# Second MLP of a two-stack block on one Trainium2 core: one 512-column matmul in place of two of 256 for the high weights

## Chip, core and metric

One core of a Trainium2 chip. The time is the device time of one execution in microseconds (us). The kernel before has three timed runs with a median of 1813.36 us.

## What is computed

The reference runs 272 tokens (16 meta tokens and 256 of input) of width 1024 through a stack of layers: a state-space mixer and an MLP, latent attention and a second MLP, then on the last 256 tokens an mLSTM mixer, cross attention, a gated MLP, a second kind of self-attention, cross attention and a gated MLP. All inputs are float32. The part that matters here is the second MLP:

```python
def sqrelu_mlp(h, w_up, w_down):
    return jnp.square(jax.nn.relu(h @ w_up)) @ w_down
h = h + sqrelu_mlp(rms_norm(h, ln_mlp[i]), mlp_w_up[i], mlp_w_down[i])
```

with `w_up` of 1024 x 4096 and `w_down` of 4096 x 1024. For i = 1 it is computed for 256 tokens only.

## The kernel before

**Layout.** Features lie on the 128 partitions and tokens in the free dimension, so the residual `X` is 8 chunks of 128 x 272. All weights come from HBM once, in blocks of up to 128 x 1024 (512 KB): 8 chunks of a 128 x 128 stationary operand that together give one output chunk of 128 features.

**Float32 out of reduced matmuls.** TensorE multiplies in a reduced float format (`F32R`). Each operand is split into a high part, which is the value rounded to that format, and a low part, the rest. A product is then high x high + high weight x low operand + low weight x high operand. For the weights ScalarE copies `RAW` to `WH` (a copy that rounds) and VectorE subtracts, `WL = RAW - WH`. For the operand, ScalarE writes `HNH` or `ASH` and VectorE `HNL` or `ASL`. `HNH/HNL` hold the normed input of the up projection (8 chunks), `ASH/ASL` the squared relu (16 chunks, two quarters of the hidden layer).

**One list of blocks.** `PLAN` is a list of all 514 weight blocks in the order of their use, and every engine's program walks it. SyncE loads block j into `RAW[j % 4]` as soon as `WL` of j-4 is written. ScalarE's `act_split` keeps three blocks ahead (`LEAD`), VectorE's `dve_split` two (`LEAD_LO`), into `WH` and `WL` with four buffers each. `pe_block` waits for the bank (one of three, i % 3, free once the eviction of block i-3 is done), for `WL` of its block and for each operand chunk, and then issues 24 matmuls with 256 (or 272) columns, three for each of 8 chunks:

```python
                q.matmul(o, wh, xh, k == 0, False)
                q.matmul(o, wh, xl, False, False)
                t = q.matmul(o, wl, xh, False, k == kc - 1)
```

The operand's part is the moving one, and the weights are the stationary one, loaded ahead of each matmul.

**The MLP.** The hidden layer is done in four quarters of 8 blocks. `mlp_order` gives the order: up 0, up 1, down 0, up 2, down 1, up 3, down 2, down 3, in all 64 blocks. In this text block n is the n-th of them, so up 0 is blocks 0 to 7 and down 0 is blocks 16 to 23. The order of each engine's instructions is that of its function's loop (`pe_mlp`, `act_mlp`, `dve_mlp`, `pool_mlp`), and each engine takes them strictly in order:

- Up block: ScalarE first splits a later block (`WH`), then waits for the matmuls and writes relu of the bank into `TMP[n % 4]`, which frees the bank. GpSimd squares `TMP` in place. ScalarE rounds it to `ASH` (`act_part`), VectorE writes `ASL` (`dve_part`). VectorE's order in a block: `WL` of a later block, then `ASL` of this one.
- Down block: VectorE writes `WL` of a later block, waits for the matmuls and multiplies the bank by the row `RR2` (the square of 1/rms, since the norm's scale is applied only here) into `TMP[6 + n % 2]`, which frees the bank. GpSimd adds that to `X`. VectorE waits for the add of two down blocks earlier before it writes into the same `TMP`.
- Up 0 also ends the norm: the sum of squares comes from TensorE behind block 0, ScalarE makes a rough 1/rms with Ln and Exp, and VectorE refines it (`dve_newton`, L171) and squares it into `RR2`.
- Down 3 also begins the next norm: `act_norm`, `dve_norm` and GpSimd's sums of pairs of squares.

The profile names the helper's line for every instruction: L140 is a matmul, L149 an activation, L159 `tensor_tensor`, L171 `scalar_tensor_tensor`, L180 `tensor_reduce`, L189 a DMA. So instructions are told apart by their tiles.

Of the kernel before, what the change touches and what calls it, by code (L numbers as in the profile page):

```python
# [5 lines left out]
ALU = mybir.AluOpType  # L6
# [5 lines left out]
T1 = 272  # L12
T2 = 256
# [186 lines left out]
def build_program(nc, cpack, xin, memin, W, out):  # L200
    with ExitStack() as ctx:

        def sb(name, shape, dt=F32):
            return ctx.enter_context(nc.sbuf_tensor(name, shape, dt))
# [6 lines left out]
        def sig(name):  # L211
            sigs.append(Sig(sem(name)))
            return sigs[-1]
# [26 lines left out]
        def row(n, T):  # L240
            return Rbuf[:, n, 0:T]
# [78 lines left out]
        def pe_block(q, name, r, m, T, xs):  # L320
            i = q.block(name, r, m)
            pe_bank_free(q, i)
            q.wait_ge(*lo[i])
            o = bank_of(i)[:, 0:T]
            kc = KC[name]
            for k in range(kc):
                xh, xl, ready = xs[k]
                wh = WH[:, i % NWS, k * 128:(k + 1) * 128]
                wl = WL[:, i % NWS, k * 128:(k + 1) * 128]
                q.wait_ge(*ready)  # L330
# [3 lines that stand above are left out]
                if k == kc - 1:  # L334
                    t.then_inc(*use(i))

        def act_block(q, name, r, m, T):
            i = q.block(name, r, m)
            act_split(q, i)
            return i, bank_of(i)[:, 0:T]  # L340
# [6 lines left out]
        def hn_chunks(key):  # L347
            T = NORMS[key][3]
            return [(HNH[:, c, 0:T], HNL[:, c, 0:T], hn[key, c]) for c in range(8)]

        def as_chunks(tag, c0, n, T, by=1):
            return [(ASH[:, c0 + c, 0:T], ASL[:, c0 + c, 0:T], al[tag, c // by]) for c in range(n)]
# [583 lines left out]
        r2 = sig("r_squared")  # L936
        sqr = sig("relu_squared")
        xadd = sig("x_added")

        MT = (T1, T2)  # L940

# [6 lines left out]
        def mlp_order():  # L948
            return [("up", 0), ("up", 1), ("down", 0), ("up", 2), ("down", 1), ("up", 3), ("down", 2), ("down", 3)]

        def pe_mlp(q, l, nxt):
            key = f"mlp{l}"
            xs = hn_chunks(key)
            for kind, q4 in mlp_order():
                for m in range(8):
                    if kind == "up":
                        pe_block(q, f"up{l}", 0, 8 * q4 + m, MT[l], xs)
                        if q4 == 0 and m == 0:
                            pe_rest(q, key, MT[l])
                    else:  # L960
                        pe_block(q, f"down{l}", q4, m, MT[l], as_chunks(("up", l, q4), q4 % 2 * 8, 8, MT[l]))
                        if q4 == 3:
                            pe_feed(q, nxt, m, NORMS[nxt][3], rms[key])

        def act_mlp(q, l, nxt):
            key, T = f"mlp{l}", MT[l]
            for kind, q4 in mlp_order():
                if kind == "down" and q4 == 3:
                    q.table(LOGS)
                for m in range(8):  # L970
                    if kind == "up":
                        n, c = 8 * q4 + m, q4 % 2 * 8 + m
                        i, b = act_block(q, f"up{l}", 0, n, T)
                        if n == 0:
                            act_table(q, key, row(RST, T), T, 1024,
                                      evd[AT["ssd", 0, 47]] if l == 0 else evd[AT["mlain", 0, 2]])
                        v = TMP[:, n % 4, 0:T]
                        q.wait_ge(*use[i])
                        if n >= 4:
                            q.wait_ge(*al[("up", l, (n - 4) // 8), (n - 4) % 8])  # L980
                        q.activation(v, b, ACT.Relu).then_inc(*eva(i))
                        act_part(q, ("up", l, q4), m, ASH[:, c, 0:T], v, up_free(l, q4), sqr[l, n])
                    else:
                        i, b = act_block(q, f"down{l}", q4, m, T)
                        if q4 == 3:
                            act_norm(q, nxt, m, xadd[l, 3, m], use[AT[f"up{l}", 0, 31]])

        def dve_mlp(q, l, nxt):
            key, T = f"mlp{l}", MT[l]
            for kind, q4 in mlp_order():  # L990
                for m in range(8):
                    if kind == "up":
                        n, c = 8 * q4 + m, q4 % 2 * 8 + m
                        if n == 0:
                            dve_norm(q, key, 7)
                        i, b = dve_block(q, f"up{l}", 0, n, T)
                        if n == 0:
                            r = row(RST, T)
                            dve_newton(q, key, r, SUMS[:, 0:T], 1024, rough[key])
                            q.wait_ge(*rms[key])  # L1000
                            if l:
                                q.wait_ge(*evd[AT["down0", 3, 7]])
                            q.tt(row(RR2, T), r, r, ALU.mult).then_inc(*r2(l))
                        dve_part(q, ("up", l, q4), m, ASL[:, c, 0:T], TMP[:, n % 4, 0:T], ASH[:, c, 0:T])
                    else:
# [3 lines left out]
                        q.wait_ge(*r2[l])  # L1009
                        if n >= 2:  # L1010
                            q.wait_ge(*xadd[l, (n - 2) // 8, (n - 2) % 8])
                        q.tt(TMP[:, 6 + n % 2, 0:T], b, row(RR2, T), ALU.mult).then_inc(*evd(i))
                        if q4 == 3 and m:
                            dve_norm(q, nxt, m - 1)

        def pool_mlp(q, l, nxt):
            T, t0 = MT[l], T1 - MT[l]
            for kind, q4 in mlp_order():
                for m in range(8):
                    if kind == "up":  # L1020
                        n = 8 * q4 + m
                        v = TMP[:, n % 4, 0:T]
                        q.wait_ge(*eva[AT[f"up{l}", 0, n]])
                        q.tt(v, v, v, ALU.mult).then_inc(*sqr(l, n))
                    else:
                        n = 8 * q4 + m
                        q.wait_ge(*evd[AT[f"down{l}", q4, m]])
# [4 lines left out]
                        q.tt(X[:, m, t0:T1], X[:, m, t0:T1], TMP[:, 6 + n % 2, 0:T], ALU.add).then_inc(*xadd(l, q4, m))  # L1032
                        if q4 == 3:
                            pool_pair(q, nxt, m, NORMS[nxt][3])

# [1693 lines left out]
```

## Time and profile before

| | |
|---|---|
| timed runs | 1811.76, 1813.36, 1814.75 us; median 1813.36 |
| the profiled execution | 1816.08 us, of which the span of the instructions is 1814.3 |
| TensorE | 1728.0 us busy (95%), 13396 matmuls; granted clock 0.965 in the mean |
| VectorE | 1193.6 us (66%), 2054 instructions |
| ScalarE | 934.8 us (52%), 1640 |
| GpSimd | 316.0 us (17%), 281 |
| HBM read | 254.29 MB, 141 GB/s over the span |
| second MLP | from about 700 us (first matmuls) to 884 us (last add to X) of the span |

Times of rows are in microseconds from the start of the span, PE is TensorE, DVE VectorE, ACT ScalarE, POOL GpSimd. A row of the timeline has the start, the duration, the engine, the line, the operation, what is written and what is read, and in brackets how long the engine had been idle before it and whom it waited for. A duration runs to the end of an instruction's last write, and the next instruction can start before that.

### The profile page before, as it was taken

How to read it: one execution, taken by the hardware profiler on the slowest of the kernel's cores; microseconds unless marked ns; L12 is line 12 of the kernel's file. 1: busy time of each engine (PE TensorE's matmuls, PEld its weight loads, DVE VectorE, ACT ScalarE, POOL GpSimd, SP SyncE). 2: the span in 40 equal slices, each digit the busy share in tenths (PEclk: the TensorE clock that was granted, in tenths of full speed). 3: DMA queues.
4: the chain of work that ended last, by engine and by line, in shares of the span. 5: the costliest groups of instructions: out<-in, count | busy, mean ns of one | idle time of the engine just before them, and what ended most of it. 6: DMA issues, size and time to landing. Idle time of an engine off the chain costs nothing.

```text
span 1814.3 us, 33107 instructions
## 1 busy us (share of the span) xinstructions
PE 1728.0 (95%) x13396; PEld 1659.1 (91%) x13396; DVE 1193.6 (66%) x2054; ACT 934.8 (52%) x1640; POOL 316.0 (17%) x281
## 2 busy tenths in 40 slices
PE   6999999999988999999999999999989999989997
PEld 6999889999986989999988999999989998889997
DVE  5899987555576446555766675776666766466665
ACT  5677765544443445544655444544445654354443
POOL 0000001233420002333211100000241211010025
PEclk8999999999998779999999999999999999999998
DMA  5333334555522116555533544455553343335553
GB/s 186 120 114 105 117 103 140 163 176 173 179 79 79 44 57 189 194 187 186 164 116 117 180 146 129 140 183 187 183 169 116 113 156 117 99 123 175 188 179 109
DMA packets 76328, 257.49 MB, mean 142 GB/s; under 512 B 8464, under 2 KB 12560, under 8 KB 75920
## 3 DMA queue, kind: packets, MB, share of 16 engines
q1 hardware_dynamic: 76176, 255.37, 43.9%
q8 instruction: 107, 1.75, 0.4%
q14 instruction: 45, 0.37, 0.1%
HBM read 254.29 MB, written 1.05 MB: 141 GB/s over the span
## 4 chain that ended last, share of the span: by engine, by line
PE 78%; DVE 11%; ACT 5%; issue 4%; POOL 1%; DMA 0%; POOLq 0%; DVEq 0%; ACTq 0%; SPq 0%
PE pb L140 77%; DVE WL L159 2%; DVE TMP L171 2%; DVE SCR L171 2%; DVE SCR L159 2%; PE pb L143 1%; ACT SCR L149 1%; ACT L156 1%; POOL SCR L159 1%; ACT WH L149 1%; DVE HNL L171 1%; ACT TMP L149 1%; ACT Rbuf L149 0%; ACT SCR L150 0%; DVE MX L180 0%
## 5 line engine op out<-in xcount | busy, mean ns | idle before, releaser
L140 PE MATMUL pb<-HNH,WH 128*128 128x256 f32 (+1 forms) x2176 | 632.8, 291 | 3.6 <-DVE WL L159 3.5
L140 PE MATMUL pb<-HNH,WL 128*128 128x256 f32 (+1 forms) x2176 | 621.7, 286 | 0.0
L140 PE MATMUL pb<-HNL,WH 128*128 128x256 f32 (+1 forms) x2176 | 621.2, 285 | 0.0
L159 DVE TENSOR_TENSOR WL<-RAW,WH 128x1024 fp32r<-128x1024 f32 (+4 forms) x514 | 602.5, 1174 | 6.8 <-ACT WH L149 6.1
L149 ACT ACTIVATE WH<-RAW 128x1024 fp32r<-128x1024 f32 (+4 forms) x514 | 507.4, 989 | 170.5 <-PE pb L140 169.0
L140 PE MATMUL pb<-ASH,WH 128*128 128x256 f32 (+1 forms) x1632 | 479.0, 294 | 3.2 <-DVE ASL L171 1.8
L140 PE MATMUL pb<-ASH,WL 128*128 128x256 f32 (+1 forms) x1632 | 469.3, 288 | 0.0
L140 PE MATMUL pb<-ASL,WH 128*128 128x256 f32 (+1 forms) x1632 | 468.8, 287 | 0.0
L140 PEld LDWEIGHTS pb<-HNH,WH 128*128 128x128 f32 x2176 | 415.6, 191 | 10.4 <-issue 4.7
L140 PEld LDWEIGHTS pb<-HNH,WL 128*128 128x128 f32 x2176 | 415.6, 191 | 0.0
L140 PEld LDWEIGHTS pb<-HNL,WH 128*128 128x128 f32 x2176 | 414.2, 190 | 1.1
L140 PEld LDWEIGHTS pb<-ASH,WH 128*128 128x128 f32 x1632 | 315.7, 193 | 10.6 <-issue 5.3
L140 PEld LDWEIGHTS pb<-ASL,WH 128*128 128x128 f32 x1632 | 315.0, 193 | 1.0
L140 PEld LDWEIGHTS pb<-ASH,WL 128*128 128x128 f32 x1632 | 315.7, 193 | 0.0
L140 PE MATMUL pb<-SCR 128*64 128x128 f32 (+11 forms) x928 | 136.2, 319 | 15.5 <-DVE SCR L171 9.5
L140 PEld LDWEIGHTS pb<-SCR 128*128 128x128 f32 (+5 forms) x928 | 105.7, 173 | 36.1 <-DVE SCR L171 11.2
L159 DVE TENSOR_TENSOR ASL<-TMP,ASH 128x256 fp32r<-128x256 f32 (+1 forms) x108 | 46.4, 430 | 109.2 <-ACT ASH L149 109.2
L140 PE MATMUL pb<-SQ,cp 128*128 128x256 f32 (+2 forms) x274 | 85.6, 428 | 33.5 <-ACT SQ L149 24.0
L159 POOL TENSOR_TENSOR SCR<-SCR,TMP 128x256 f32<-128x256 f32 x48 | 59.9, 1248 | 311.7 <-DVE TMP L159 311.7
L159 POOL TENSOR_TENSOR X<-X,TMP 128x272 f32<-128x272 f32 (+1 forms) x64 | 96.4, 1507 | 87.9 <-DVE TMP L159 87.9
L159 DVE TENSOR_TENSOR TMP<-pb,Rbuf 128x256 f32<-128x256 f32 (+1 forms) x112 | 47.9, 428 | 94.8 <-PE pb L140 94.8
L149 ACT ACTIVATE ASH<-TMP 128x256 fp32r<-128x256 f32 (+1 forms) x108 | 45.5, 422 | 117.2 <-DVE TMP L159 67.6
(136 smaller groups left out, 1484.8 us busy)
## 6 DMA issues: line engine op xcount, KB each, us to landing
RAW<-in_w_gu SPq DMA_DIRECT2D x88, 512.0 KB, 4.1
RAW<-in_w_up SPq DMA_DIRECT2D x64, 512.0 KB, 3.5
RAW<-in_w_down SPq DMA_DIRECT2D x64, 512.0 KB, 3.6
RAW<-in_w_ssd SPq DMA_DIRECT2D x48, 512.0 KB, 3.5
RAW<-in_w_xkv SPq DMA_DIRECT2D x32, 512.0 KB, 3.5
RAW<-in_w_mlin SPq DMA_DIRECT2D x24, 512.0 KB, 3.5
RAW<-in_w_fd SPq DMA_DIRECT2D x32, 384.0 KB, 3.0
RAW<-in_w_sbqkv SPq DMA_DIRECT2D x24, 512.0 KB, 3.9
```

The source lines that it names most:

```text
L140: return self.eng.matmul(o, l, r, start=start, stop=stop, skip_group_check=skip) if self.eng else Nothing()
L143: return self.eng.transpose(o, i, ident) if self.eng else Nothing()
L149: return self.eng.activation(o, i, f, bias=bias, scale=scale)
L156: self.eng.preload_act_table_set(name)
L159: return self.eng.tensor_tensor(o, a, b, op) if self.eng else Nothing()
L171: return self.eng.scalar_tensor_tensor(out=o, in0=a, scalar=s, in1=b, op0=op0, op1=op1)
```

## The change

In the second MLP (l = 1) the up blocks and the down blocks of quarters 0 to 2 take another form; the first MLP and down 3 stay.

- `HNH/HNL` become the two halves of one tile `HN[:, chunk, 0 or 1, token]`, and `ASH/ASL` those of `AS`, so that the high and the low part of a chunk lie 272 columns apart.
- `pe_wide_block`: for each chunk one matmul of 512 columns with the stationary `WH`, whose moving operand is the high part and then the low part, 256 columns each, into both halves of the bank; then one of 256 columns with `WL` and the high part, into the first half. So 16 matmuls a block instead of 24, and the block's result is the sum of the bank's halves.
- Whoever reads the bank adds the halves. That is VectorE with a `tensor_reduce` over a view of the bank whose last dimension has two elements, 256 apart.
- Up block: VectorE does that reduction into `TMP`, which now frees the bank; ScalarE then does relu in place in `TMP`, GpSimd's square follows. `ASH` and `ASL` of block n are written one block later (`act_square_part`, `dve_square_part` of n-1, after the relu and the reduction of n), except at a quarter's last block, which ScalarE writes in the same block and VectorE at the start of the next group.
- Down block (quarters 0 to 2): the reduction takes the place of VectorE's product with `RR2`; GpSimd multiplies by `RR2` in place, waits for its own product, and then adds to `X`.

The core of the diff:

```diff
-        HNH = sb("HNH", [128, 8, T1], F32R)
-        HNL = sb("HNL", [128, 8, T1], F32R)
-        ASH = sb("ASH", [128, 16, T1], F32R)
-        ASL = sb("ASL", [128, 16, T1], F32R)
+        HN = sb("HN", [128, 8, 2, T1], F32R)
+        AS = sb("AS", [128, 16, 2, T1], F32R)
+        HNH, HNL = HN[:, :, 0, :], HN[:, :, 1, :]
+        ASH, ASL = AS[:, :, 0, :], AS[:, :, 1, :]
...
-                q.wait_ge(*(eva if PLAN[i - 3][0] in ("up0", "up1", "wk") else evd)[i - 3])
+                q.wait_ge(*(eva if PLAN[i - 3][0] in ("up0", "wk") else evd)[i - 3])
...
+        def pe_wide_block(q, name, r, m, xs):
...
+            for k in range(kc):
+                x, ready = xs[k]
+                q.wait_ge(*ready)
+                q.matmul(o[:, :].rearrange("p (a t) -> p a t", a=2), WH[:, i % NWS, k * 128:(k + 1) * 128], x[:, :, 0:T2],
+                         k == 0, False, True)
+                t = q.matmul(o[:, 0:T2], WL[:, i % NWS, k * 128:(k + 1) * 128], x[:, 0, 0:T2], False, k == kc - 1, True)
+            t.then_inc(*use(i))
+
+        def halves(b):
+            return b[:, :].rearrange("p (a t) -> p t a", a=2)
...
                         v = TMP[:, n % 4, 0:T]
-                        q.wait_ge(*use[i])
-                        if n >= 4:
-                            q.wait_ge(*al[("up", l, (n - 4) // 8), (n - 4) % 8])
-                        q.activation(v, b, ACT.Relu).then_inc(*eva(i))
-                        act_part(q, ("up", l, q4), m, ASH[:, c, 0:T], v, up_free(l, q4), sqr[l, n])
+                        if l:
+                            q.wait_ge(*evd[i])
+                            q.activation(v, v, ACT.Relu).then_inc(*relu(n))
...
+                            if m:
+                                act_square_part(q, l, n - 1)
+                            if m == 7:
+                                act_square_part(q, l, n)
...
-                        dve_part(q, ("up", l, q4), m, ASL[:, c, 0:T], TMP[:, n % 4, 0:T], ASH[:, c, 0:T])
+                        v = TMP[:, n % 4, 0:T]
+                        if l:
+                            q.wait_ge(*use[i])
+                            if n >= 4:
+                                q.wait_ge(*al[("up", l, (n - 4) // 8), (n - 4) % 8])
+                            q.red(v, halves(bank_of(i)), ALU.add, False).then_inc(*evd(i))
+                        if l == 0:
+                            dve_square_part(q, l, n)
+                        elif m or q4 == 1:
+                            dve_square_part(q, l, n - 1)
                     else:
                         i, b = dve_block(q, f"down{l}", q4, m, T)
+                        if l and m == 0 and q4 < 3:
+                            dve_square_part(q, l, 15 if q4 == 0 else 8 * q4 + 15)
...
+                        if down_wide(l, q4):
+                            q.red(v, halves(bank_of(i)), ALU.add, False).then_inc(*evd(i))
+                        else:
+                            q.wait_ge(*r2[l])
+                            q.tt(v, b, row(RR2, T), ALU.mult).then_inc(*evd(i))
...
+                        if down_wide(l, q4):
+                            q.wait_ge(*r2[l])
+                            q.tt(v, v, row(RR2, T), ALU.mult).then_inc(*scaled(q4, m))
+                            q.wait_ge(*scaled[q4, m])
```

## Rows read from the trace of the kernel before

**Rows 1.** The chain that ended last, in order of time, 700 to 890 us: start, us, what.

```profile
by line: PE pb L140 100.1%
...
699.95 190.11 PE pb L140 x1595
```

**Rows 2.** Two stretches: us, then PE, PEld, DVE, ACT, POOL busy, PEclk, DMA share, GB/s.

```profile
716.00:860.00 144.00, 144.00 (x1219) 144.00 (x1218) 79.46 (x103) 73.22 (x107) 54.71 (x51) 1.00 0.58 188
900.00:960.00 60.00, 55.57 (x426) 52.90 (x427) 38.94 (x68) 32.78 (x51) 6.80 (x5) 1.00 0.39 124
```

**Rows 3.** Timeline of PE: first matmul of blocks 3 and 17 (start us, us).

```profile
709.05 0.28 PE L140 MATMUL pb<-HNH,WH 128*128 128x256 f32 x1
...
748.81 0.28 PE L140 MATMUL pb<-ASH,WH 128*128 128x256 f32 x1
```

**Rows 4.** Timeline of DVE, up blocks: start us, us, what [idle before].

```profile
781.81 0.43 DVE L159 TENSOR_TENSOR ASL<-TMP,ASH 128x256 fp32r<-128x256 f32 x1 [1.28 <-ACT ASH L149]
782.15 1.22 DVE L159 TENSOR_TENSOR WL<-RAW,WH 128x1024 fp32r<-128x1024 f32 x1
```

**Rows 5.** Timeline of DVE, the turn from up to down blocks.

```profile
748.07 1.22 DVE L159 TENSOR_TENSOR WL<-RAW,WH 128x1024 fp32r<-128x1024 f32 x1
749.21 0.42 DVE L159 TENSOR_TENSOR TMP<-pb,Rbuf 128x256 f32<-128x256 f32 x1
```

**Rows 6.** Timeline of PE: V projection, first and last of 24 matmuls of 512 columns.

```profile
563.70 0.39 PE L140 MATMUL pb<-WH,ASH 128*128 128x512 f32 x1
...
569.03 0.40 PE L140 MATMUL pb<-WL,ASH 128*128 128x512 f32 x1
```

**Rows 7.** Timeline of ACT: the norm before block 1, and one up block.

```profile
704.08 0.42 ACT L149 ACTIVATE Rbuf<-Rbuf 128x256 f32<-128x256 f32 x1
...
780.25 0.38 ACT L149 ACTIVATE TMP<-pb 128x256 f32<-128x256 f32 x1 [0.36 <-PE pb L140]
781.36 0.42 ACT L149 ACTIVATE ASH<-TMP 128x256 fp32r<-128x256 f32 x1 [0.72 <-POOL TMP L159]
781.68 1.04 ACT L149 ACTIVATE WH<-RAW 128x1024 fp32r<-128x1024 f32 x1
```

**Rows 8.** Groups of DVE over the whole run: xcount | busy us, mean ns.

```profile
L180 DVE TENSOR_REDUCE SCR<-pb 128x1 f32<-128x272 f32 x16 | 6.9, 430 | 0.0
L180 DVE TENSOR_REDUCE MX<-pb 128x2 f32<-128x512 f32 x8 | 5.5, 691 | 5.0 <-PE pb L140 5.0
L171 DVE SCALAR_TENSOR_TENSOR SCR<-pb,cp 128x512 f32<-128x512 f32 x8 | 6.0, 750 | 10.2 <-PE pb L140 10.2
```

**Rows 9.** Timeline of POOL: the square of block 0, and one in up 2.

```profile
704.85 0.61 POOL L159 TENSOR_TENSOR TMP<-TMP 128x256 f32<-128x256 f32 x1 [8.97 <-ACT TMP L149]
...
780.71 0.61 POOL L159 TENSOR_TENSOR TMP<-TMP 128x256 f32<-128x256 f32 x1 [2.23 <-ACT TMP L149]
```

**Rows 10.** Timeline of DVE: the Newton step before the first eviction.

```profile
704.99 0.75 DVE L171 SCALAR_TENSOR_TENSOR TMP<-TMP,Rbuf 128x256 f32<-128x256 f32 x1
705.78 0.43 DVE L171 SCALAR_TENSOR_TENSOR Rbuf<-TMP,Rbuf 128x256 f32<-128x256 f32 x1
...
706.58 0.42 DVE L159 TENSOR_TENSOR ASL<-TMP,ASH 128x256 fp32r<-128x256 f32 x1
```

**Rows 11.** Timeline of DVE in down 3.

```profile
869.03 1.76 DVE L159 TENSOR_TENSOR WL<-RAW,WH 128x1024 fp32r<-128x1024 f32 x1
```

**Rows 12.** Timeline of POOL: adds to X in down 0 and down 3.

```profile
749.71 1.65 POOL L159 TENSOR_TENSOR X<-X,TMP 128x256 f32<-128x256 f32 x1 [2.46 <-DVE TMP L159]
...
868.79 0.91 POOL L159 TENSOR_TENSOR X<-X,TMP 128x256 f32<-128x256 f32 x1 [0.24 <-DVE TMP L159]
```

**Rows 13.** DMA issues: xcount, KB each, median us from issue to landing.

```profile
RAW<-in_w_up SPq DMA_DIRECT2D x64, 512.0 KB, 3.5
```

More of the change, by code:

```diff
@@ L335, in pe_block @@
                     t.then_inc(*use(i))
+        def pe_wide_block(q, name, r, m, xs):
+            i = q.block(name, r, m)
+            pe_bank_free(q, i)
+            q.wait_ge(*lo[i])
+            o = bank_of(i)
+            kc = KC[name]
+            for k in range(kc):
[7 more added lines that the diff above has]
+            return b[:, :].rearrange("p (a t) -> p t a", a=2)
         def act_block(q, name, r, m, T):
@@ L349, in hn_chunks, with hn_wide, as_wide @@
             return [(HNH[:, c, 0:T], HNL[:, c, 0:T], hn[key, c]) for c in range(8)]
+        def hn_wide(key):
+            return [(HN[:, c], hn[key, c]) for c in range(8)]
+        def as_wide(tag, c0, n, by=1):
+            return [(AS[:, c0 + c], al[tag, c // by]) for c in range(n)]
         def as_chunks(tag, c0, n, T, by=1):
@@ L938, in build_program @@
         xadd = sig("x_added")
+        relu, scaled = sig("relu"), sig("down_scaled")
         MT = (T1, T2)
@@ L949, in mlp_order, with down_wide @@
             return [("up", 0), ("up", 1), ("down", 0), ("up", 2), ("down", 1), ("up", 3), ("down", 2), ("down", 3)]
+        def down_wide(l, q4):
+            return l == 1 and q4 < 3
         def pe_mlp(q, l, nxt):
             key = f"mlp{l}"
-            xs = hn_chunks(key)
+            xs = hn_wide(key) if l else hn_chunks(key)
             for kind, q4 in mlp_order():
@@ L956, in pe_mlp @@
                     if kind == "up":
-                        pe_block(q, f"up{l}", 0, 8 * q4 + m, MT[l], xs)
+                        if l:
+                            pe_wide_block(q, "up1", 0, 8 * q4 + m, xs)
+                        else:
+                            pe_block(q, "up0", 0, 8 * q4 + m, T1, xs)
                         if q4 == 0 and m == 0:
                             pe_rest(q, key, MT[l])
+                    elif down_wide(l, q4):
+                        pe_wide_block(q, "down1", q4, m, as_wide(("up", l, q4), q4 % 2 * 8, 8))
                     else:
@@ L963, in pe_mlp, with act_square_part, dve_square_part @@
                             pe_feed(q, nxt, m, NORMS[nxt][3], rms[key])
+        def act_square_part(q, l, n):
+            q4, m = divmod(n, 8)
+            act_part(q, ("up", l, q4), m, ASH[:, q4 % 2 * 8 + m, 0:MT[l]], TMP[:, n % 4, 0:MT[l]], up_free(l, q4), sqr[l, n])
+        def dve_square_part(q, l, n):
+            q4, m = divmod(n, 8)
+            c = q4 % 2 * 8 + m
+            dve_part(q, ("up", l, q4), m, ASL[:, c, 0:MT[l]], TMP[:, n % 4, 0:MT[l]], ASH[:, c, 0:MT[l]])
         def act_mlp(q, l, nxt):
@@ L971, in act_mlp @@
                     if kind == "up":
[L972 removed]
+                        n = 8 * q4 + m
                         i, b = act_block(q, f"up{l}", 0, n, T)
@@ L992, in dve_mlp @@
                     if kind == "up":
-                        n, c = 8 * q4 + m, q4 % 2 * 8 + m
+                        n = 8 * q4 + m
                         if n == 0:
@@ L1003, in dve_mlp @@
                             q.tt(row(RR2, T), r, r, ALU.mult).then_inc(*r2(l))
-                        dve_part(q, ("up", l, q4), m, ASL[:, c, 0:T], TMP[:, n % 4, 0:T], ASH[:, c, 0:T])
+                        v = TMP[:, n % 4, 0:T]
+                        if l:
+                            q.wait_ge(*use[i])
+                            if n >= 4:
+                                q.wait_ge(*al[("up", l, (n - 4) // 8), (n - 4) % 8])
+                            q.red(v, halves(bank_of(i)), ALU.add, False).then_inc(*evd(i))
+                        if l == 0:
+                            dve_square_part(q, l, n)
+                        elif m or q4 == 1:
+                            dve_square_part(q, l, n - 1)
                     else:
                         i, b = dve_block(q, f"down{l}", q4, m, T)
+                        if l and m == 0 and q4 < 3:
+                            dve_square_part(q, l, 15 if q4 == 0 else 8 * q4 + 15)
                         n = 8 * q4 + m
                         q.wait_ge(*use[i])
-                        q.wait_ge(*r2[l])
                         if n >= 2:
                             q.wait_ge(*xadd[l, (n - 2) // 8, (n - 2) % 8])
-                        q.tt(TMP[:, 6 + n % 2, 0:T], b, row(RR2, T), ALU.mult).then_inc(*evd(i))
+                        v = TMP[:, 6 + n % 2, 0:T]
+                        if down_wide(l, q4):
+                            q.red(v, halves(bank_of(i)), ALU.add, False).then_inc(*evd(i))
+                        else:
+                            q.wait_ge(*r2[l])
+                            q.tt(v, b, row(RR2, T), ALU.mult).then_inc(*evd(i))
                         if q4 == 3 and m:
@@ L1022, in pool_mlp @@
                         v = TMP[:, n % 4, 0:T]
-                        q.wait_ge(*eva[AT[f"up{l}", 0, n]])
+                        q.wait_ge(*(relu[n] if l else eva[AT["up0", 0, n]]))
                         q.tt(v, v, v, ALU.mult).then_inc(*sqr(l, n))
@@ L1026, in pool_mlp @@
                         n = 8 * q4 + m
+                        v = TMP[:, 6 + n % 2, 0:T]
                         q.wait_ge(*evd[AT[f"down{l}", q4, m]])
+                        if down_wide(l, q4):
+                            q.wait_ge(*r2[l])
+                            q.tt(v, v, row(RR2, T), ALU.mult).then_inc(*scaled(q4, m))
+                            q.wait_ge(*scaled[q4, m])
                         if q4:
@@ L1031, in pool_mlp @@
                             q.wait_ge(*evd[AT["ssdo", 1, m] if l == 0 else AT["mlao", 0, m]])
-                        q.tt(X[:, m, t0:T1], X[:, m, t0:T1], TMP[:, 6 + n % 2, 0:T], ALU.add).then_inc(*xadd(l, q4, m))
+                        q.tt(X[:, m, t0:T1], X[:, m, t0:T1], v, ALU.add).then_inc(*xadd(l, q4, m))
                         if q4 == 3:
```

4 lines of the change are left out of this document (added).

## The prediction

> **What bounds the kernel now.** I read the page first, then the chain of waits over the second MLP, then that stage's timeline engine by engine. The chain runs on TensorE alone for 190 us [rows 1], and TensorE is busy in all of 716 to 860 us at a granted clock of 1.00, that is at 2.4 GHz, while VectorE works 55% of it and ScalarE 51% [rows 2]. So only TensorE's own time, or something that newly holds it up, can move the result. The stage has 64 blocks: 32 up, 32 down. One block is 24 matmuls of 256 columns. From the first matmul of block 3 (709.05) to the first of block 17 (748.81) there are 14 blocks [rows 3], so a block takes 39.76 / 14 = 2.84 us and a matmul 118.3 ns. The 0.28 in these rows is how long one takes from end to end; successive matmuls overlap.
>
> VectorE's rows show how much room it has: in an up block it subtracts WL (1.22 us), then sits idle for 1.28 us until ScalarE's ASH, then writes ASL (0.42) [rows 4]. The eviction is ScalarE's, and VectorE is not in it. In a row of VectorE the next instruction starts before the last ends: ASL at 781.81 and WL at 782.15 are 0.34 apart, and WL 748.07 to TMP 749.21 is 1.14 [rows 4, 5]. I use 0.34, 1.14 and a lead of 0.08 us.
>
> **The change on TensorE.** 56 blocks (32 up, 24 down) turn two 256-column matmuls per chunk into one of 512: eight pairs a block. The 512-column matmuls of this trace are those of the V projection: from 563.70 to 569.03 there are 23 steps [rows 6], 231.7 ns each. The pair costs 236.6 ns now. Eight times 4.9 ns is 0.04 us a block, so a block takes 2.80 us, and 56 blocks save 2.2 us. That is all that TensorE gives: the columns stay the same, and the only thing saved is a fixed share per matmul. The bounds are 0 (the same rate per column) and, since 512 columns at 2.4 GHz need 213 ns, 8 x (236.6 - 213.3) = 0.19 us a block or 10.4 us; I take the row, because it is the same width with its weights loaded each time. The Trainium skill (TensorE: Matmul & The Clock Gate, Back-to-back issue gap) puts the gap at N/2.4 + 2.5 ns: by it a pair would save 2.5 ns and the stage 1.1 us. The rows don't follow it, neither at 256 columns (118.3) nor at 512 (231.7).
>
> **The change off TensorE.** In an up block ScalarE's relu out of the bank (0.38) becomes VectorE's reduction of 512 elements into TMP, then a relu from TMP to TMP, which I price at 0.42 as ScalarE's other SBUF copies of 256 [rows 7]. No row has a reduction of pairs; the reduction of 512 bank elements into two takes 691 ns, of 272 into one 430 [rows 8]. So it goes by elements read, and I take 0.69, occupying VectorE for 0.61. Bounds: 0.60, and 1.22, the price of 1,024 elements, should each of the 256 outputs cost something. In a down block the reduction replaces a product of 0.42, and the product moves to GpSimd as one more instruction in front of the add to X.
>
> **The new ring.** The reduction is not free, because each step of an up block now waits for another engine, and VectorE stands in that queue twice. Counted from the start of reduction n: it ends at 0.69; relu n at 0.73 to 1.15; ScalarE starts ASH of n-1 0.32 us after relu (as from ASH to WH [rows 7]), 1.05 to 1.47; VectorE could write ASL of n-1 at 1.50. But GpSimd squares v of n from 1.23 (0.08 after ScalarE [rows 7, 9]) to 1.84, and the two exclude each other: with GpSimd's square at 704.85 to 705.46 VectorE's step at 704.99 took 0.75 where the next takes 0.43, and ended 0.28 after GpSimd's [rows 9, 10]; WL at 869.03 took 1.76 for 1.22 beside the add to X at 868.79 [rows 11, 12]. So ASL ends at 1.84 + 0.28 = 2.12, WL starts at 2.04 and reduction n+1 at 3.18. **3.18 against TensorE's 2.80: VectorE sets the up blocks**, 0.38 us a block, once its lag has used the buffers up.
>
> **How much lag there is.** WL of block n+3 is ready 2.04 + 1.22 + 0.05 = 3.31 after reduction n. The banks are no limit: reduction n frees the bank of n+3 after 0.74. The first reduction waits behind the Newton step of the norm, after which VectorE starts its next instruction at 706.58 [rows 10]; less 0.32, because the square no longer lies beside that step, 706.26. Block 0 has no ASL before it, so reduction 1 starts at 706.26 + 0.61 + 1.14 = 708.01, and n at 708.01 + 3.18 (n-1). TensorE wants block n+3 at 708.93 + 2.80 n (709.05 less three blocks' gain). For n = 2 it is 714.50 against 714.53; from n = 3 TensorE waits, 0.34 and then 0.38 for n = 4 to 7: 1.9 us. Reduction 8 is followed by ASL of 7, which ScalarE has written already: 0.61 + 0.34 + 1.14 = 2.09, so VectorE gains 1.09 once. That covers nearly three blocks, and five more pay 0.38: another 1.9 us. Up 2 and up 3 start without lag, since a down block asks 1.75 of VectorE (at most 0.54 more beside GpSimd [rows 11]). Six steps of 0.38 make 2.28 at their end, where 5.60 - 0.20 - 3.31 = 2.09 is free: 0.2 us each. Stalls: 1.9 + 1.9 + 0.4 = 4.2 us. **Sum: -2.2 + 4.2 = +2.0 us.**
>
> The rest costs nothing here. GpSimd in a down block: its product starts at 0.77 under WL and ends about 0.47 after it, 2.30; the add then takes about 0.75 outside WL, so X is added by 3.1, and reduction n+2, which waits for it, starts at 5.6. Without WL's shadow an add took 0.91, under it 1.65 [rows 12]. ScalarE has 1.9 us of work in 3.18. Loads need RAW, which WL frees up to 3 us later; they land in 3.5 us [rows 13] and have three blocks' lead. The clock: short holes don't lower it, 900 to 960 us has TensorE busy 93% at 1.00 [rows 2].
>
> The profiled execution took 1816.08 us for a span of 1814.3, while the runs' median is 1813.36; I put the difference on the median: 1815.4. About 0.2% (3.6 us) is what a measurement of this kernel can tell from no change.
>
> **Rivals.**
> (a) TensorE still sets everything: if GpSimd's square does not hold ASL, the ring is 3.18 - 0.21 = 2.97, over 2.80 by 0.17 only, and stalls shrink to about 1 us: -1.2 us; with none, -2.2. For: reduction and relu keep VectorE free while the square starts. Against: rows 10. Within 0.2% either way: 0.14.
> (b) **Slower: the pair reduction is dearer than 0.69.** Place: the head of the ring. Each 0.01 us of it is paid by some 14 blocks of the first two groups and, once the lag outruns 2.09, by some 8 in each of up 2 and up 3: 0.3 us. It decides from 0.745 us on (+3.6 us); at 0.85 it gives +6.8, at 1.0 +11. For: 256 outputs instead of two, input 256 elements apart; other 512-element readers of a bank take 0.75 [rows 8]. Against: 430 and 691 fit one rate. 0.27.
> (c) Faster: the wide matmul comes near its 213 ns. Then a block takes 2.65 and 10.4 us are saved, but the ring exceeds it by 0.53: 13 blocks of the first two groups pay that, less the 1.1, plus 0.5 of start-up, 6.3 us, and up 2 and up 3 overrun 1.79 us of room by 1.4 each: -1.3 us. With a reduction of 0.60 besides, -4 us, 1809. It needs both: 0.08.
> (d) VectorE's instructions don't overlap behind waits: two handovers of 0.08 make the ring 3.34, 15 blocks pay 0.16 more, and up 2 and up 3 overrun by 1.2 us each: +6.5 us. Against: in rows 5 a product with a wait starts 1.14 after a WL of 1.22. The Trainium skill (VectorE: DVE Perf Modes, The DRAIN you can't avoid) has the next instruction start only once the pipe is empty, and would give this; the trace contradicts it. 0.05.
> The forecast itself has 0.46.
>
> **How the numbers follow.** Forecast and (a) are within 0.2%: 0.60. (b) and (d): 0.32 slower. (c): 0.08 faster. The range takes in (a), most of (c) and (b) up to a reduction of 0.95 us: 1810 to 1823.
>
> **What would show it.** 512-column matmuls of HN and AS 0.232 apart, at 448 of them; the reduction at 0.69 in VectorE's list; in 716 to 750 blocks 3.18 apart, with short idle of TensorE put down to WL; ASL at 0.6 instead of 0.42 beside the square; up 2 nearly free of stalls, its blocks 2.80 apart, and 2.80 in the down blocks too; GpSimd at some 20 us more busy time. It is wrong if the ring stays under 2.9 us, if TensorE waits for banks rather than WL, if GpSimd's chain holds VectorE in the down blocks, or if the clock falls in the up blocks.

## The result, and the profile after

| | before | after |
|---|---|---|
| median of 22 runs | 1813.98 us (1811.76 to 1818.29) | 1818.63 us (1811.65 to 1824.3) |
| ratio of the times | | 1.0024, 95% interval 1.0014 to 1.0034 |
| a later set: 35 and 12 runs | 1814.36 us | 1815.42 us (1812.52 to 1821.99), ratio 1.0011, 0.9999 to 1.0024 |
| profiled execution, its span | 1816.08, 1814.3 us | 1814.1, 1812.3 us |
| second MLP, by the split's blocks | 184.91 us | 186.75 us |
| first MLP, by the split's blocks | 197.02 us | 196.14 us |

In the medians the change costs 0.24% in the first set and 0.11% in the second, whose interval takes in no change at all. The profiled execution of the changed kernel is by chance shorter than that of the kernel before, although the changed stage in it is longer: whole runs differ by more than the change is worth, and the stage has to be read by itself. I measure it between two of ScalarE's copies RAW to WH: that of the first block of the second MLP (index 169 in the list of blocks, `PLAN`) and that of the first block behind it (233). I call this the stage time. Timeline of ScalarE in the profile before, at blocks 65 and 129 (the first MLP between them), 169 and 233:

```profile
307.72 1.05 ACT L149 ACTIVATE WH<-RAW 128x1024 fp32r<-128x1024 f32 x1
...
504.74 1.05 ACT L149 ACTIVATE WH<-RAW 128x1024 fp32r<-128x1024 f32 x1
...
691.23 1.05 ACT L149 ACTIVATE WH<-RAW 128x1024 fp32r<-128x1024 f32 x1
...
876.14 1.04 ACT L149 ACTIVATE WH<-RAW 128x1024 fp32r<-128x1024 f32 x1
```

The same four rows of the changed kernel:

```profile
307.18 1.04 ACT L149 ACTIVATE WH<-RAW 128x1024 fp32r<-128x1024 f32 x1
...
503.32 1.04 ACT L149 ACTIVATE WH<-RAW 128x1024 fp32r<-128x1024 f32 x1
...
688.95 1.04 ACT L149 ACTIVATE WH<-RAW 128x1024 fp32r<-128x1024 f32 x1
...
875.70 1.04 ACT L149 ACTIVATE WH<-RAW 128x1024 fp32r<-128x1024 f32 x1
```

The chain of waits of the changed kernel over 700 to 890 us, where [rows 1] had TensorE alone (start, us, what):

```profile
by line: PE pb L140 74.8%; DVE WL L159 9.4%; issue 5.7%; DVE TMP L180 4.5%; ACT AS L149 2.8%; DVE AS L159 1.1%; ACT Rbuf L149 0.5%; DVE TMP L171 0.5%; ACT TMP L149 0.4%; DVE Rbuf L171 0.2%; DVE Rbuf L159 0.2%
...
708.90 0.61 DVE TMP L180
710.29 0.63 DVE AS L159
710.92 1.14 DVE WL L159
712.06 0.61 DVE TMP L180
...
747.67 1.22 DVE WL L159
749.03 3.03 PE pb L140 x16
752.19 45.03 PE pb L140 x256
```

Up to 749 us the chain goes round reduction, ASL, WL, and from 752 us on it is TensorE again. ("issue" in the first line is time in which an engine waited for nothing that the profile shows.) So VectorE sets the time in up 0 and up 1, and hardly in up 2 and up 3. One turn of the ring on VectorE (answers to [rows 4]):

```profile
711.98 0.68 DVE L180 TENSOR_REDUCE TMP<-pb 128x256 f32<-128x512 f32 x1
713.45 0.64 DVE L159 TENSOR_TENSOR AS<-TMP,AS 128x256 fp32r<-128x256 f32 x1 [0.79 <-ACT AS L149]
714.00 1.22 DVE L159 TENSOR_TENSOR WL<-RAW,WH 128x1024 fp32r<-128x1024 f32 x1
715.14 0.68 DVE L180 TENSOR_REDUCE TMP<-pb 128x256 f32<-128x512 f32 x1
```

on ScalarE ([rows 7]):

```profile
712.69 0.42 ACT L149 ACTIVATE TMP<-TMP 128x256 f32<-128x256 f32 x1 [1.48 <-DVE TMP L180]
713.01 0.40 ACT L149 ACTIVATE AS<-TMP 128x256 fp32r<-128x256 f32 x1
```

and on GpSimd ([rows 9]):

```profile
713.19 0.61 POOL L159 TENSOR_TENSOR TMP<-TMP 128x256 f32<-128x256 f32 x1 [2.54 <-ACT TMP L149]
```

From reduction to reduction it is 3.16 us. I call this way round the ring: VectorE's reduction, ScalarE's relu and ASH, VectorE's ASL and WL, and the next reduction. VectorE sits idle for 0.79 while ScalarE does relu and ASH, and then ASL takes 0.64 instead of 0.42 because the square, 713.19 to 713.80, lies over its start at 713.45. TensorE's wide blocks (timeline, two pairs in block 4, where nothing holds them, then the wait before block 5):

```profile
713.33 0.39 PE L140 MATMUL pb<-HN,WH 128*128 128x512 f32 x1
713.56 0.28 PE L140 MATMUL pb<-HN,WL 128*128 128x256 f32 x1
713.68 0.39 PE L140 MATMUL pb<-HN,WH 128*128 128x512 f32 x1
...
714.96 0.28 PE L140 MATMUL pb<-HN,WL 128*128 128x256 f32 x1
715.37 0.47 PE L140 MATMUL pb<-HN,WH 128*128 128x512 f32 x1
```

A pair of 512 and 256 columns takes 0.35 us, eight of them 2.80; the first matmul of block 5 comes 0.41 after the last of block 4, where 0.12 is usual. By the semaphore that TensorE raises at the end of each block, blocks 5 to 9 and 13 to 17 end 3.11 to 3.21 us after the one before, the second blocks of down 1 and down 2 3.04, and all other wide blocks 2.79 to 2.85.

Busy time by stretch (us, then PE, PEld, DVE, ACT, POOL, clock, DMA share, GB/s), up 0 and 1, then down 0, up 2, down 1:

```profile
716.00:750.00 34.00, 32.98 (x179) 27.15 (x178) 25.76 (x33) 18.87 (x35) 7.56 (x11) 1.00 0.53 172
750.00:771.00 21.00, 20.88 (x119) 18.08 (x118) 16.43 (x19) 9.87 (x11) 18.01 (x16) 1.00 0.66 221
771.00:794.00 23.00, 23.00 (x133) 20.16 (x133) 17.17 (x22) 11.43 (x20) 7.07 (x9) 1.00 0.49 164
794.00:817.00 23.00, 22.99 (x132) 19.93 (x131) 17.63 (x20) 10.35 (x12) 18.96 (x16) 1.00 0.66 206
```

The granted clock is 1.00 in all four, that is 2.4 GHz. GpSimd is 18 of 21 us busy in down 0 and does hold VectorE up: in each of down 0, 1 and 2 five reductions wait some 0.70 us for an add to X. TensorE doesn't feel it, its blocks in down 0 stay 2.80 apart.

### The profile page after: what moved, and what is told of

The parts are those of the page before. It is cut to its first block, busy times and chain, and to the rows that moved or that the text cites. A ratio compares the mean times of both kernels' runs of the same rounds, so it can differ in the third digit from the quotient of the medians.

```text
span 1812.3 us, 32299 instructions
## 1 busy us (share of the span) xinstructions
PE 1723.0 (95%) x12948; PEld 1633.3 (90%) x12948; DVE 1228.9 (68%) x2086; ACT 932.6 (51%) x1640; POOL 335.5 (19%) x305
## 4 chain that ended last, share of the span: by engine, by line
PE 77%; DVE 12%; ACT 5%; issue 4%; POOL 1%; DMA 0%; POOLq 0%; SPq 0%; ACTq 0%; DVEq 0%
PE pb L140 75%; DVE WL L159 3%; DVE TMP L171 2%; DVE SCR L171 2%; DVE SCR L159 2%; PE pb L143 2%; ACT L156 1%; POOL SCR L159 1%; ACT SCR L149 1%; DVE HN L171 1%; ACT WH L149 1%; ACT AS L149 1%; ACT TMP L149 1%; DVE TMP L180 0%; ACT Rbuf L149 0%
## 5 line engine op out<-in xcount | busy, mean ns | idle before, releaser
L140 PE MATMUL pb<-HN,WH 128*128 128x256 f32 (+2 forms) x4096 | 812.4, 295 | 5.7 <-DVE WL L159 4.6
L140 PEld LDWEIGHTS pb<-HN,WH 128*128 128x128 f32 x4096 | 652.9, 191 | 26.4 <-issue 8.5
L140 PE MATMUL pb<-HN,WL 128*128 128x256 f32 (+1 forms) x2176 | 622.4, 286 | 0.0
L140 PE MATMUL pb<-AS,WH 128*128 128x256 f32 (+2 forms) x3072 | 616.7, 298 | 3.6 <-DVE AS L171 1.8
L140 PEld LDWEIGHTS pb<-AS,WH 128*128 128x128 f32 x3072 | 497.2, 194 | 21.8 <-issue 7.4
L140 PE MATMUL pb<-AS,WL 128*128 128x256 f32 (+1 forms) x1632 | 469.9, 288 | 0.0
L140 PEld LDWEIGHTS pb<-HN,WL 128*128 128x128 f32 x2176 | 413.9, 190 | 0.1
L140 PEld LDWEIGHTS pb<-AS,WL 128*128 128x128 f32 x1632 | 315.3, 193 | 0.0
L149 ACT ACTIVATE TMP<-TMP 128x256 f32<-128x256 f32 (+1 forms) x132 | 55.5, 421 | 165.4 <-DVE TMP L171 117.8
L159 DVE TENSOR_TENSOR AS<-TMP,AS 128x256 fp32r<-128x256 f32 (+1 forms) x108 | 52.2, 483 | 89.6 <-ACT AS L149 89.6
L159 POOL TENSOR_TENSOR X<-X,TMP 128x272 f32<-128x272 f32 (+1 forms) x64 | 92.6, 1447 | 55.4 <-DVE TMP L159 53.5
```

Source lines behind the costliest of these rows:

```text
L140: return self.eng.matmul(o, l, r, start=start, stop=stop, skip_group_check=skip) if self.eng else Nothing()
L149: return self.eng.activation(o, i, f, bias=bias, scale=scale)
L159: return self.eng.tensor_tensor(o, a, b, op) if self.eng else Nothing()
```

## The experiments

The stage time below is always that between blocks 169 and 233 of the split; the table at the end of this section puts it beside the whole runs.

**The changed kernel again (e1_again).** 

> The changed kernel once more, unchanged. In the profile that I have, the second MLP (from the split of the first block of up 0's lead to the turn out of down 3) takes 1.8 us more than before, while the median of 22 runs is 4.7 us up and single runs reach 10 us. Theory T (the ring through VectorE sets the up blocks, 3.16 us against 2.80): the stage is again 1.8 us longer where the clock stays at 1.00. Theory C (the holes that the ring makes in TensorE's work now and then let its clock fall to 0.5 in the up blocks): an execution with a time above 1818 has spells of clock 0.50 between 700 and 770 us that the short ones don't have. Rival D: the lost clock lies elsewhere and the stage is 1.8 us longer in all of them.

1815.42 us, stage 186.75, clock 1.00 in it. The profile was of a run at 1813.2, so it doesn't decide between C and D; a profile of a long execution follows below.

**ASL two blocks late (e2_late_low).** VectorE's order in an up block is WL of n+2, ASL of n-2, reduction of n.

```diff
+                            if m > 1 or q4 == 1:
+                                dve_square_part(q, l, n - 2)
                             q.wait_ge(*use[i])
...
                             q.red(v, halves(bank_of(i)), ALU.add, False).then_inc(*evd(i))
...
-                        elif m or q4 == 1:
-                            dve_square_part(q, l, n - 1)
```

> The whole change, but VectorE writes ASL of block n-2, ahead of the reduction of n, instead of ASL of n-1 behind it. Then nothing that VectorE does in an up block waits for ScalarE's answer to the reduction of the same block. Theory T: the ring falls from 3.16 to about 0.61 + 1.14 + 0.34 = 2.1 us, TensorE sets the up blocks at 2.80 and the stage is 2.2 us shorter than before: about 1811.5, ratio 0.9988. Theory C: also no clock spells, so the spread of the runs is that of the kernel before. Rival (TensorE pays something for the wide form that isn't in the ring): no better than the changed kernel.

Stage 182.64 us, 2.27 less than before. The order of VectorE alone removes every stall: the wide blocks of up 0 to up 3 all end 2.80 apart. Timeline, a stretch in which VectorE still catches up:

```profile
712.71 0.68 DVE L180 TENSOR_REDUCE TMP<-pb 128x256 f32<-128x512 f32 x1
713.31 1.21 DVE L159 TENSOR_TENSOR WL<-RAW,WH 128x1024 fp32r<-128x1024 f32 x1
714.45 0.83 DVE L159 TENSOR_TENSOR AS<-TMP,AS 128x256 fp32r<-128x256 f32 x1
715.20 0.68 DVE L180 TENSOR_REDUCE TMP<-pb 128x256 f32<-128x512 f32 x1
```

The turn is 2.49 and not the 2.1 that I expected: GpSimd's square now runs beside WL, 713.92 to 715.00, and ASL takes 0.83, to 715.28, again 0.28 after it; it is below 2.80, and that suffices. But the whole runs did not get shorter: 1814.21 against 1814.36 us, ratio 1.0002 (0.9992 to 1.0011). Theory T held for the stage and failed for the kernel.

**Only the up blocks (e3_up_only)**, and **only the down blocks (e4_down_only).** The first:

```diff
-            return l == 1 and q4 < 3
+            return False
```

and the second, whose up blocks also have the evictions of the kernel before (not shown):

```diff
-            xs = hn_wide(key) if l else hn_chunks(key)
+            xs = hn_chunks(key)
...
-                        if l:
-                            pe_wide_block(q, "up1", 0, 8 * q4 + m, xs)
-                        else:
-                            pe_block(q, "up0", 0, 8 * q4 + m, T1, xs)
+                        pe_block(q, f"up{l}", 0, 8 * q4 + m, MT[l], xs)
```

> Only the up blocks take the wide form, the down blocks are as before. Theory T: stalls 3.8 us in the first two groups and 0.4 in up 2 and up 3, as in the changed kernel, gain 32 x 0.04 = 1.3 us: stage +2.9 us. Theory C: the spread and the extra of the median over the profile stay. Rival (GpSimd's doubled work in the down blocks carries the loss): near 0.

> Only the down blocks of quarters 0 to 2 take the wide form, the up blocks are as before. Theory T: 24 x 0.04 = 1.0 us less than before, no stall; ratio 0.9995. Theory C: no added spread. Rival (GpSimd's product and add hold VectorE's reduction and so the bank): slower than before by 1 us or more, with VectorE waiting for the add to X.

Stages 187.47 (+2.56, where I expected +2.9) and 183.90 (-1.01, as expected). The loss sits in the up blocks, and GpSimd's second instruction in the down blocks costs the stage nothing. Together they make +1.55 where the whole change has +1.84, so they nearly add. Whole runs: 1818.91 us, ratio 1.0027 (1.0015 to 1.0040), and 1812.92 us, 0.9995 (0.9984 to 1.0006).

**No square on GpSimd (e5_no_square).** The hidden layer is relu instead of its square, and ScalarE's ASH waits for relu alone.

```diff
-            act_part(q, ("up", l, q4), m, ASH[:, q4 % 2 * 8 + m, 0:MT[l]], TMP[:, n % 4, 0:MT[l]], up_free(l, q4), sqr[l, n])
+            act_part(q, ("up", l, q4), m, ASH[:, q4 % 2 * 8 + m, 0:MT[l]], TMP[:, n % 4, 0:MT[l]], up_free(l, q4), relu[n] if l else sqr[l, n])
...
-                        q.wait_ge(*(relu[n] if l else eva[AT["up0", 0, n]]))
-                        q.tt(v, v, v, ALU.mult).then_inc(*sqr(l, n))
+                        if l == 0:
+                            q.wait_ge(*eva[AT["up0", 0, n]])
+                            q.tt(v, v, v, ALU.mult).then_inc(*sqr(l, n))
```

> The changed kernel without GpSimd's square in the second MLP (the hidden layer is relu, not its square): left out is one product of 256 elements a block. It measures the clash between the square and ASL by itself. Theory T: ASL takes 0.42 again instead of 0.63 and starts as early, so the ring is 3.16 - 0.21 = 2.95; the first two groups lose some 13 x 0.21 us less, and up 2 and up 3 stay free of stalls: stage 2.5 to 3 us shorter than the changed kernel's (190.0 us in the profiles I have), about 187.2. Rival (the chain over ScalarE alone makes the ring): 3.16 stays.

ASL is back at 0.43 and the turn at 2.96 us (timeline of VectorE):

```profile
717.24 0.69 DVE L180 TENSOR_REDUCE TMP<-pb 128x256 f32<-128x512 f32 x1
718.72 0.43 DVE L159 TENSOR_TENSOR AS<-TMP,AS 128x256 fp32r<-128x256 f32 x1 [0.79 <-ACT AS L149]
719.06 1.22 DVE L159 TENSOR_TENSOR WL<-RAW,WH 128x1024 fp32r<-128x1024 f32 x1
720.20 0.69 DVE L180 TENSOR_REDUCE TMP<-pb 128x256 f32<-128x512 f32 x1
```

So the clash was 0.20 of the ring's 3.16. The stage, from 691.68 to 875.05, is 183.37, which is 3.4 us less than the changed kernel's (I had written 190.0 for that in the expectations, by another end point; by the same two copies it is 186.75). Whole runs: 1812.71 us, ratio 0.9988 (0.9978 to 0.9998).

**TensorE's part alone (e6_pe_only).** The 56 wide blocks, evicted out of the bank's first half by the instructions of the kernel before, `b` being `bank_of(i)[:, 0:T]`. What it leaves out is the product of the operand's low part with the high weights, which lies in the other half. Of the edit, the down blocks' eviction:

```diff
-                        if down_wide(l, q4):
-                            q.red(v, halves(bank_of(i)), ALU.add, False).then_inc(*evd(i))
-                        else:
-                            q.wait_ge(*r2[l])
-                            q.tt(v, b, row(RR2, T), ALU.mult).then_inc(*evd(i))
+                        q.wait_ge(*r2[l])
+                        q.tt(v, b, row(RR2, T), ALU.mult).then_inc(*evd(i))
```

> TensorE's part alone: the wide matmuls in the same 56 blocks, but evicted as before, by ScalarE's relu in up blocks and VectorE's product in down blocks, out of the first half of the bank. Left out is the low part of the operand times the high weights. Theory: the ceiling of the change, 56 x 0.04 = 2.2 us off the stage of 188.2, that is 186.0, as with ASL written later. Rival (wide matmuls cost more on TensorE when their bank is read by halves): less. If the clock elsewhere doesn't answer to the stage's length, the median goes down by the same 2.2 us.

Stage 182.64 us, to the hundredth that of ASL two blocks late. So 2.27 us is what the wide matmuls give, and 186.75 - 182.64 = 4.11 us is what the stalls take. Whole runs: 1814.62 us, ratio 1.0005 (0.9995 to 1.0015). Only the wide matmuls and the tiles' layout differ from before here, and the 2.3 us are missing from the runs.

**Only the layout (e7_layout)**, and **a long execution of the changed kernel (e8_again).** The first has both edits of the up-only and the down-only kernel at once, so that of the change only the interleaved tiles HN and AS are left.

> Only the tiles HN and AS with the high and low part 272 columns apart; all matmuls and evictions as before. Open question: the changed kernel's runs spread up to 1824 us, those before only to 1818, and in a profile at 1821 us TensorE's clock was at half for 27 us from 652 us on, ahead of the changed code. Theory L (the layout brings that on): this kernel's runs spread to 1820 and above as often. Rival G (it goes with the moment at which stages meet the clock's changes, which the stage's length moves): this kernel's runs lie where those before lie, ratio 1.000.

> One more look at the changed kernel, to see in a profile where clock is lost. If its time is above 1818: spells of clock 0.50 that the profiles at 1813 and 1814 don't have; in the second MLP under theory C, before or behind it under D. The stage is 190.0 us long either way under D.

The layout alone: 1815.98 us (1812.56 to 1821.12), ratio 1.0011 (1.0000 to 1.0021), second MLP 184.89 as before, first MLP 196.14. The other profile is of an execution of 1820.62 us. Its second MLP is 186.74 at a clock of 1.00, as in the others; C has fallen and D stands. What is longer is the stretch ahead of it, the end of the latent attention. 652 to 676 us in this execution (columns as above):

```profile
652.00:676.00 24.00, 22.35 (x100) 19.02 (x99) 6.51 (x24) 7.96 (x27) 0.00 (x0) 0.59 0.00 0
```

in that of the layout alone (1817.3 us):

```profile
652.00:676.00 24.00, 21.94 (x89) 18.55 (x88) 5.44 (x21) 7.90 (x26) 0.00 (x0) 0.55 0.00 0
```

and in the first profile of the changed kernel (1814.1 us):

```profile
652.00:676.00 24.00, 21.61 (x134) 19.31 (x134) 8.55 (x27) 9.45 (x30) 0.00 (x0) 0.86 0.04 9
```

The same 24 us hold 100, 89 or 134 matmuls, at a granted clock of 0.59, 0.55 or 0.86. Between the copies of blocks 161 and 169, the attention's output projection, it makes 59.2, 60.7 and 53.3 us. The instructions of this stretch are the same in all these kernels; only HN and AS lie elsewhere than before. TensorE does the cores of the attention in it, small matmuls with waits for ScalarE and VectorE between them.

The stretch ahead of it, from block 129 to 161, has to be added. The five profiles with interleaved tiles and 53 us behind take 131.8 to 132.4 us for it, all others 129.9 to 130.2. From 129 to 169 the interleaved kernels so take 185.3 to 185.7 or 189.1 to 190.6 us, and those with the old places 183.5 to 186.5. The profile of TensorE alone has 185.3 us here: 1.8 more than the shortest with the old places, against 2.3 saved in the second MLP and 0.9 in the first. The table at the end of this section leaves this stretch out.

**The kernel before as a control (e9_control, and one execution each in e10_control and e11_control).**

> The kernel before, submitted as a kernel of its own: what the measurement makes of no change, and a second profile of it. Rival G (the long spell of half clock at the end of the latent attention comes by the execution, not by the layout): the runs spread as in the kernel before and now and then one profile shows the spell of 24 to 27 us from about 652 us. Theory L (it comes with the tiles 272 columns apart): no such spell in any profile of this kernel, and none of its runs above 1818 or so.

> A look at the kernel before, for one more profile: under G the end of the latent attention (eight blocks of the split) takes 53, 56 or 60 us from one profile to the next, under L never 60. The second MLP takes 184.9 us by the split's blocks either way.

> As the look before it: the same two forecasts, for a third profile of the kernel before on this chip.

1813.38 us, ratio 0.9993 (0.9984 to 1.0002), and the single executions 1816.20 and 1811.51; the stretch from 161 to 169 took 53.8, 55.1 and 53.3 us, 56.5 in the first profile; never 60. Second MLP 184.91 in all four, first MLP 197.02 in all four.

**ASL two blocks late, with the parts in their old places (e12_late_old_layout).**

```diff
-        HN = sb("HN", [128, 8, 2, T1], F32R)
-        AS = sb("AS", [128, 16, 2, T1], F32R)
-        HNH, HNL = HN[:, :, 0, :], HN[:, :, 1, :]
-        ASH, ASL = AS[:, :, 0, :], AS[:, :, 1, :]
+        HN = sb("HN", [128, 2, 8, T1], F32R)
+        AS = sb("AS", [128, 2, 16, T1], F32R)
+        HNH, HNL = HN[:, 0, :, :], HN[:, 1, :, :]
+        ASH, ASL = AS[:, 0, :, :], AS[:, 1, :, :]
...
-            return [(HN[:, c], hn[key, c]) for c in range(8)]
+            return [(HN[:, :, c], hn[key, c]) for c in range(8)]
```

`as_wide` changes likewise, and VectorE's order is that of e2_late_low.

> The change with ASL two blocks late, and with the high and low parts in the places that they have in the kernel before: all high chunks 272 columns apart, then all low ones, so that the moving operand's two halves are 2176 (HN) or 4352 (AS) columns apart. Theory L: what costs in whole runs is the interleaved layout, by way of the clock in the latent attention. Then the first MLP takes 197.0 us again by the split's blocks (196.1 with the interleaved tiles), the end of the latent attention 53 to 57, the second MLP 182.6 against 184.9, runs stay under 1818, and the median is 2 us under the kernel before: ratio 0.9988. Rival G: as ASL two blocks late alone, ratio 1.000, with some runs above 1818.

**1811.79 us (1809.56 to 1814.56), ratio 0.9987 (0.9978 to 0.9996)**: shorter than the kernel before by 0.13%. The interval is clear of no change, but the step is smaller than the 0.2% that I had put as what can be told. The first MLP takes 197.02 again, the stretch from 161 to 169 53.4, and the stage 182.28 us, from here to here:

```profile
688.63 1.04 ACT L149 ACTIVATE WH<-RAW 128x1024 fp32r<-128x1024 f32 x1
...
870.91 1.04 ACT L149 ACTIVATE WH<-RAW 128x1024 fp32r<-128x1024 f32 x1
```

Its chain over 700 to 890 us is TensorE's again (start, us, what):

```profile
by line: PE pb L140 99.0%; issue 0.7%; ACT SCR L149 0.4%; DVE SCR L159 0.2%; DVE SCR L174 0.2%; DVE SCR L165 0.1%; ACT L149 0.0%
...
699.89 188.03 PE pb L140 x1159
```

| kernel | second MLP | 161 to 169 in its profile | median | highest |
|---|---|---|---|---|
| before (and the control, four profiles) | 184.91 | 53.3 to 56.5 | 1813.4 to 1815.0 | 1818.6 |
| after (three profiles) | 186.75 | 53.3, 53.4, 59.2 | 1818.6, 1815.4 | 1824.3 |
| late ASL | 182.64 | 53.3 | 1814.2 | 1821.0 |
| up only | 187.47 | 60.7 | 1818.9 | 1824.3 |
| down only | 183.90 | 53.3 | 1812.9 | 1819.9 |
| no square | 183.37 | 60.7 | 1812.7 | 1817.4 |
| TensorE alone | 182.64 | 53.5 | 1814.6 | 1820.9 |
| layout alone | 184.89 | 60.7 | 1816.0 | 1821.1 |
| late ASL, old places | 182.28 | 53.4 | 1811.8 | 1814.6 |

The mean granted clock of every execution is on record too, and it gives the comparison on the same chip. The sets of the seven kernels with interleaved tiles, e1_again to e7_layout, were taken on two chips, and a set of the kernel before was taken beside them on each. A clock of 0.962 or lower was granted in 40 of 81 executions of the seven and in 3 of 64 of the kernel before. The control and late ASL in the old places ran on two further chips, with 1 of 22. The mean doesn't say where in a run the clock was lost: late ASL's profile has 0.962 and yet only 53.3 us from 161 to 169.

## Why the prediction was right, and where it was not

**TensorE's saving.** I had 2.2 us, from 231.7 ns for 512 columns. TensorE alone gave 2.27. The steps of 0.23 and 0.12 us in the timeline are those of [rows 3, 6]. The Trainium skill (TensorE: Matmul & The Clock Gate, Back-to-back issue gap) gives N/2.4 + 2.5 ns as the gap of a matmul by itself. I had applied it to this stream of weight loads and matmuls, where it would have left half of the saving, and the same rows don't follow it.

**The ring.** 3.18 forecast, 3.16 measured, and part by part: reduction 0.68 (0.69), ScalarE's ASH 0.40 (0.42), ASL 0.64 beside the square (I had it end 0.28 after the square, and it ended 713.45 + 0.64 = 714.09, 0.29 after 713.80), WL started 0.55 after ASL, and the lead of VectorE's next instruction stayed 0.08. Taking away one of its links (the square) shortened it by 0.20, and taking away a dependence (ASL two blocks late) to 2.49, less far than the 2.1 expected. Rival (d), that VectorE's instructions don't overlap, is gone: in the ring WL starts 0.09 before ASL's end. The Trainium skill (VectorE: DVE Perf Modes, The DRAIN you can't avoid) has the next instruction start only when the pipe is empty, but adds: "A next op that is not held starts earlier". The prediction passed over that, and the rows here agree with it.

**The reduction of pairs.** The point on which slower hung, rival (b): 0.684 us in the mean of 56, no dearer for 256 sums of two elements 256 apart than the 0.691 for two outputs.

**The stalls.** 4.2 forecast, 4.11 measured. They come at the places named. By the ends of TensorE's blocks, set against TensorE alone, 3.64 us fall on two rows of five blocks of some 0.36, with three blocks between them that the 1.09 of block 8 pays for (1.9 + 1.9 forecast, each row one block later), and 0.23 each are left by up 2 and up 3 for the down block behind them (0.2 forecast).

**Rival (c)** fell with the saving. Rival (a) fell with ASL's 0.63. GpSimd's part was wrong, and it is one of the signs that I had named: X was to be added long before the reduction that waits for it. In catching up VectorE runs ahead of TensorE, and in each of down 0 to down 2 it waited some 0.70 us five times for that add. It cost nothing, since TensorE was not held by it and the lag was gone by the next up group.

**The step that failed is "the rest costs nothing here".** The stage is up by 1.84 us (2.0 forecast), but the median of 22 runs by 4.65, which puts that set at 0.24%, in the case slower that I gave 0.32 and not in the likeliest one. The second set is up by 1.06 only, 0.11%, and that its 1815.42 is the forecast 1815.4 is luck: the forecast stood on a median of three runs and had nothing of the tiles in it. I had counted the new tiles HN and AS as free. They are not: with them alone, and every matmul and eviction as before, the median stood 1.5 us above before, with an interval that just reaches no change. As far as the profiles show, it is the clock in the latent attention that gives those kernels their long executions. The long spell was in four of nine profiles of kernels with the interleaved tiles, those of the executions at 1815.8 to 1821.0 us, while the other five took 1811.6 to 1814.1; it was in none of five with the old places. Four of these five profiles are from other chips, but the counts of the granted clock above, 40 of 81 against 3 of 64, are not. Six of the seven kernels that have those tiles have runs above 1818.6, the highest in any set of the kernel before. With the parts moved back and all else kept, the median went from 0.15 us under its own set of the kernel before to 2.09 under, where the stage gave 0.4 and the first MLP took 0.9 back. The intervals of these two ratios overlap a little. That the layout brings on the spell is thus supported by both directions of the exchange, but by what path isn't shown. It could be that the interleaved tiles let the first MLP run 0.88 us shorter and the attention then starts at another point in its course of the clock; the start of the attention varies by more than that from one execution to the next, which speaks against so simple a reading. I leave it open.

## What to carry to other kernels

The wider matmul left the columns unchanged and saved only a few ns per instruction, here 5 ns a pair, while its price was paid by whoever reads the bank. Before an eviction is moved to another engine, write down the ring that it closes: VectorE, which takes its instructions in order and waited for the answer to its own last one, was bound here by the sum of the latencies, 3.16 us a turn with 0.79 of it idle, and not by its busy time; one more block of delay between question and answer removed 4.1 us without removing any work. And a change of a tenth of a per cent has to be judged at the stage and over many runs, since one profile of each can show it with the wrong sign.

## What I had not expected of the hardware

The places of the tiles set TensorE's rate by a little. In the first MLP, whose 64 blocks of 272 columns are the same instructions in all kernels, these blocks took 197.02 us with the high chunks 272 columns apart (five profiles) and 196.14 with high and low interleaved (nine profiles), which is 0.57 ns for each of 1536 matmuls; successive ones start 126.0 and 125.5 ns apart in the mean in the first profiles before and after. In the wide blocks it goes the other way: 182.28 us with the two halves far apart, 182.64 with them 272 columns apart.

TensorE's clock stayed at its lower level (1.2 GHz) for 24 to 27 us on end in the attention in four profiles, in a stretch in which TensorE is busy most of the time by the records, as in the row with 0.59 above: 22.35 of 24 us. In the row with 0.86 it is busy 21.61. The busy time of such a stretch doesn't tell the two cases apart; the number of matmuls in it does.
